# Selected attention on one core: score products between the steps of a weight chunk, a third turning buffer, and one chunk moved forward

## The chip, the cores and the metric

The kernel runs on one core of one Trainium2 chip. The metric is the device time of one launch in microseconds, the median of three runs; lower is better.

## The reference, cut to what matters

Two transformer blocks are computed for 512 tokens of width 1024 in fp32. The part around the change is in the second block: attention over compressed blocks and over selected and windowed keys (with 512 tokens all blocks are selected), eight query heads in two key groups.

```python
q = rmsnorm(q.reshape(b, s, G, R, dh), q_norm_g) * (dh ** -0.5)
s_c = jnp.einsum('bsgrd,bcgd->bgrsc', q, kc).astype(jnp.float32) + bias_c
p_c = masked_softmax(s_c, dist_c >= 0, axis=-1)
o_cmp = jnp.einsum('bgrsc,bcgd->bsgrd', p_c, vc)
```

The selected and the windowed branch do the same with their own keys and values, and a gate sums the three. Beside it, and independent of it, `h @ w_in` is needed for the RWKV projections (14 column tiles) and for two gates (16 column tiles).

## The kernel before, in words

Everything is written by hand, engine by engine; each engine runs its list in order and waits on semaphores.

**Weights come in chunks.** A chunk is 128 output columns of a weight matrix, 128 x 1024 values. SyncE loads it into one of four places of `w_raw` (L332), GpSimd splits it into `w_hi` and `w_lo` (L444, L446), and `chunk` on TensorE (L520 to L536) multiplies it in eight steps of three 512-column matmuls: L531, L532, L533. `chunk` can call a function `also` after each step.

**Fills.** The 30 chunks of the RWKV projections and the gates (f0 to f29) are spread as `fill` calls (L758) over the attention stage and the start of the RWKV stage. ScalarE copies each result out in `fill_out` (L1375, copy L1385) and stores it to DRAM (L1387).

**Units.** The attention has eight units (n, g): query tile n = 0 to 3, key group g = 0, 1. For unit u:

- `nsa_scores` (L837) makes ten products, i = 0 to 9. The first eight (L846) contract 64 rows: a query head (`qn`) against 128(n+1) key columns (`kd`). Heads alternate between partitions 0 to 63 and 64 to 127. Products 8 and 9 (L853) are against the compressed keys, two small matmuls each. The fp32 matmul is issued as two passes, so the trace has two records for each matmul. Four banks take the products in turn; product i waits until VectorE has masked product i - 4 (L843).
- VectorE adds bias and mask in `nsa_mask` (L1962, L1970), ScalarE takes the exponentials (L1441, L1447), and VectorE scales by the weights in `nsa_weights` (L1995, L1998). VectorE's order is weights of u, then mask of u + 1.
- `nsa_weigh` (L861) takes the 2(n+1) + 1 key tiles of the unit one by one: `turn_item` transposes four heads (L879), ScalarE copies the bank to `p2T` (L1462), and `sum_item` multiplies with the values (L893). There are two banks (4 and 5) and two places in `p2T`, and TensorE turns one item ahead.

The order on TensorE is set by this loop:

```python
nsa_scores(*units[0], 0)
fill()
for u, (n, g) in enumerate(units):
    if u + 1 < len(units):
        nsa_scores(*units[u + 1], u + 1)
    fill()
    nsa_weigh(n, g, u)
```

ScalarE follows with the exponentials of u + 1, the copy of the fill, then the copies of u. Before the loop stands one `fill` (f13, L833), behind it `fill(3)`, four `lora` products (L920, L921), `fill(1)`, `head_sums(0)` (L927, L930) and `fill(3)`; then the RWKV scores (L952), which wait for the last fill to be copied (L1058). The last `LATE` = 7 fills go to banks and places of their own (`late_stage`).

Of the kernel before, what the change touches and what calls it, by code (L numbers as in the profile page):

```python
# [78 lines left out]
RW_GROUPS = ((0, 2), (2, 5), (5, 8), (8, 11), (11, 14))  # L79


NFILL, LATE = 14 + 2 * KD, 7
NUNIT = 2 * NT
NORMS = (("ffn1", KD), ("mix", KD), ("pool", 4), ("attn", 4), ("ffn2", KD), ("nsa", KD), ("conv", KD))
RSQRTS = (("ffn1_in", 1), ("ffn1_post", 1), ("mix_in", 1), ("pool_in", 1), ("attn_in", 1), ("wout_post", 1),
# [30 lines left out]
def build(nc, x, positions, params, const, mix_const, w_pool, w_ffn1_gu, w_ffn1_down, w_in, w_out, w_ffn2_gu,  # L116
          w_ffn2_down, w_nsa, nsa_const, rel_bias, distance_code, cmp_pe, cmp_w1, cmp_w2,
          w_rwkv, rwkv_const, rwkv_w2a2, rwkv_g2, w_gates, w_merge, w_out_2, w_conv_up, w_conv_down, out):
    with ExitStack() as ctx:
# [99 lines left out]
        with ExitStack() as scope:  # L219

            with ExitStack() as early:
                def in_e(name, shape, dt=F32):
                    return early.enter_context(nc.sbuf_tensor(name, shape, dt))
                zn = in_e("zn", [P, 11, S])
                pair = in_e("pair", [P, 2, 2, S // 2])
                code = in_e("code", [33, 5 * P])
                rv = in_e("rv", [NH, 5 * P])


            cmp_blocks = [zn[:, a:a + 2, :].rearrange("p a b -> p (a b)")[:, 0:32 * NCMP]  # L230
                          .rearrange("p (j g b) -> p j g b", j=16, g=2) for a in (4, 2)]
            E = in_a("E", [P, 2, 8, S])
            with ExitStack() as early:
                cw1 = early.enter_context(nc.sbuf_tensor("cw1", [P, 16, CMP_H], F32))


            toeplitz = in_a("toeplitz", [P, NH, S])
            qn = in_a("qn", [P, 4, S])
            kd = in_a("kd", [P, 4, S])
            v2_tok = in_a("v2_tok", [P, 2, NT, P])  # L240
            p2T = in_a("p2T", [P, 2, 4, P])
            oA = in_a("oA", [P, 4, S])
            ncs = in_a("ncs", [P, 4 * P])
# [12 lines left out]

            stat = in_a("stat", [P, 2, 3, 12])

        def fill_bank(f):

            return 4 + f % 4 if f < 14 else 7 if f < NFILL - LATE else (0, 1, 2, 4, 5, 3, 0)[f - NFILL + LATE]

        def by_tile(x):
            return x.rearrange("p (n t) -> p n t", n=NT)
# [253 lines left out]
        @block.tensor  # L518
        def _(pe):
            def chunk(c, s, k0, k1, rhs_hi, rhs_lo, dst, start, stop, each=None, w0=None, also=None,  # L520
                      shift=0):


                w0 = k0 if w0 is None else w0
                pe.wait_ge(*nth("w_split", c + 1))
                for k in range(k0, k1):
                    if each:
                        pe.wait_ge(*nth(each, k + 1 + shift))
                    hi = w_hi[:, s, (k - w0) * P:(k - w0 + 1) * P]
                    lo = w_lo[:, s, (k - w0) * P:(k - w0 + 1) * P]  # L530
                    nc.tensor.matmul(dst, hi, rhs_hi[:, k, :], start=start and k == k0, stop=False)  # L531
                    nc.tensor.matmul(dst, hi, rhs_lo[:, k, :], start=False, stop=False)  # L532
                    last = nc.tensor.matmul(dst, lo, rhs_hi[:, k, :], start=False, stop=stop and k == k1 - 1)  # L533
                    if also:
                        also(k)
                return last  # L536
# [218 lines left out]

            filled = [0]

            def fill(n=1):  # L758

                for f in range(filled[0], filled[0] + n):  # L760
                    if f == NFILL - 1:
                        pe.wait_ge(*nth("fill_read", NFILL - LATE + 1))
                    elif 4 <= f <= NFILL - LATE:
                        pe.wait_ge(*nth("fill_read", f - 3 if f < 14 else f))
                    chunk(FIRST["rwkv"] + f, (FIRST["rwkv"] + f) % RING, 0, KD, h_hi, h_lo,
                          bank[fill_bank(f)][:, :], True, True).then_inc(sem("w_used"), 1)
                filled[0] += n

            pe.wait_ge(*nth("zn_read", 11))
# [34 lines left out]
            for v in range(2):  # L804
# [21 lines left out]
                else:  # L826
# [3 lines left out]
                                                    cw2[:, 1, h, 0:HD], start=(h == 0), stop=(h == 1),  # L830
                                                    skip_group_check=True)
                    last.then_inc(sem("nsa_job"), 1)
            fill()  # L833
            pe.wait_ge(*nth("nsa_read", 17))
            pe.wait_ge(*nth("kc_normed", 1))

            def nsa_scores(n, g, unit):  # L837


                for i in range(10):  # L840
# [20 lines left out]
            def nsa_weigh(n, g, unit):  # L861
# [8 lines left out]

                def turn_item(x):
                    v, j = items[x]
                    k = turn[0] + x
                    if k >= 2:
                        pe.wait_ge(*nth("p2T_ready", k - 1))
                    for h in range(4):
                        src = Ec[:, unit % 2, h, 0:8 * n + 7] if v == 2 else E[:, unit % 2, 4 * v + h, j * P:(j + 1) * P]
                        rows = 8 * n + 7 if v == 2 else P
                        last = nc.tensor.transpose(bank[4 + k % 2][0:rows, h * P:(h + 1) * P], src, flip)  # L879
                    last.then_inc(sem("nsa_turned"), 1)  # L880

                def sum_item(x):
# [3 lines left out]
                    for h in range(4):  # L886
                        e, i = h % 2, h // 2
                        if v == 2:
                            lhs, rhs = vct[0:8 * n + 7, g, :], p2T[0:8 * n + 7, k % 2, h, :]
                        else:  # L890
                            lhs, rhs = v2_tok[:, v, j, 64 * g:64 * g + 64], p2T[:, k % 2, h, :]
# [4 lines left out]
                    return last  # L896

                turn_item(0)
                for x in range(len(items)):
                    if x + 1 < len(items):  # L900
                        turn_item(x + 1)
                    last = sum_item(x)
                turn[0] += len(items)

            units = [(n, g) for n in range(NT) for g in range(2)]
            nsa_scores(*units[0], 0)
            fill()
# [295 lines left out]
        def _(act):  # L1203
# [209 lines left out]
            for v in range(2):  # L1413
# [13 lines left out]
                else:  # L1427
# [4 lines left out]
                    fill_out(2)  # L1432

            logs()

# [17 lines left out]
            def nsa_copies(n, g, unit):  # L1453
                items = 2 * (n + 1) + 1
                c0 = 2 * P * (unit % 2)
                for x in range(items):
                    k = turn[0] + x
                    act.wait_ge(*nth("nsa_turned", k + 1))
                    if k >= 2:
                        act.wait_ge(*nth("p2T_used", k - 1))  # L1460
                    rows = 8 * n + 7 if x == items - 1 else P
                    nc.scalar.activation(p2T[0:rows, k % 2, :, :].rearrange("p h t -> p (h t)"),  # L1462
                                         bank[4 + k % 2][0:rows, :], ACT.Copy).then_inc(sem("p2T_ready"), 1)
# [65 lines left out]
            decays(0)  # L1529
            fill_out(1)  # L1530
            key_norm(0)
            fill_out(3)
            key_rates(1)
            flat = lambda x: x.rearrange("p a b -> p (a b)")

# [839 lines left out]
```

## Time and profile before

| | |
|---|---|
| median of three runs | 2064.92 us (2062.79 to 2067.34) |
| the profiled execution | 2061.17 us |
| its span | 2059.4 us |
| TensorE busy | 1906.2 us (93%) |
| VectorE busy | 859.3 us (42%) |
| ScalarE busy | 426.5 us (21%) |
| GpSimd busy | 1278.9 us (62%) |
| chain that ended last | PE 82%, DVE 12%, ACT 3% |

The profile gives the busy time of each engine, the chain of work that ended last, the waits, and each instruction with its start. Times in the rows are from the start of the span. PE is TensorE's matmuls, PEld its weight loads, DVE VectorE, ACT ScalarE, POOL GpSimd. A matmul record's length is longer than the distance to the next, since matmuls are pipelined; costs are read from starts. The attention units lie between 1190 and 1344 us.

### The profile page before, as it was taken

Reading aid. Unit: us, or ns where it says so; the run is one execution under the profiler, and the core shown is the slowest. Engines: PE = TensorE matmul, PEld = TensorE weight load, DVE = VectorE, ACT = ScalarE, POOL = GpSimd, SP = SyncE. Lnnn points to the kernel's source line nnn. Section 1 sums busy time; section 2 is a strip of 40 time slices with the busy share of each in tenths; the row PEclk is TensorE's granted clock in tenths of the full one; section 3 lists DMA queues with packets and bytes.
Section 4 is the critical chain, followed back from the end, with each engine's and each line's share of the span. In section 5 each row is a group of like instructions: output and inputs, shape, how many; then the busy total and the mean of one; then the engine's idle time right before and its main releaser. Section 6 shows DMA issues by size and latency. Waiting matters only on the chain.

```text
span 2059.4 us, 29817 instructions
## 1 busy us (share of the span) xinstructions
PE 1906.2 (93%) x11700; PEld 1482.6 (72%) x11700; DVE 859.3 (42%) x1426; ACT 426.5 (21%) x862; POOL 1278.9 (62%) x619
## 2 busy tenths in 40 slices
PE   7999999888779999999799989997868799999998
PEld 5888888656557888888477866676755678888887
DVE  4333321267664333311404244357756635555301
ACT  3000000123431000000213145534431021111100
POOL 6888877734066888877375442333364667777773
PEclk9999999989989999999899999999968999999999
DMA  4222223311022222233242421140023222223231
GB/s 149 92 92 98 93 86 94 118 35 59 11 82 72 92 92 93 92 96 97 99 160 98 160 100 53 42 149 8 4 109 112 72 82 92 92 92 93 91 95 59
DMA packets 58780, 180.33 MB, mean 88 GB/s; under 512 B 6931, under 2 KB 13843, under 8 KB 58172
## 3 DMA queue, kind: packets, MB, share of 16 engines
q1 hardware_dynamic: 49132, 165.83, 24.0%
q10 hardware_dynamic: 9552, 13.13, 1.8%
q8 instruction: 72, 1.18, 0.2%
q14 instruction: 24, 0.20, 0.0%
HBM read 165.81 MB, written 13.13 MB: 87 GB/s over the span
## 4 chain that ended last, share of the span: by engine, by line
PE 82%; DVE 12%; ACT 3%; issue 2%; DMA 0%; ACTq 0%; POOL 0%; DVEq 0%; SPq 0%; POOLq 0%
PE bank L531 23%; PE bank L533 23%; PE bank L532 23%; PE bank L893 1%; DVE h_lo L1643 1%; PE bank L846 1%; PE bank L581 1%; PE bank L879 1%; DVE xT L1690 1%; DVE tmp L1687 1%; DVE sq L2205 1%; PE bank L810 1%; DVE m_lo L2206 1%; DVE sq L2202 1%; PE bank L1051 1%
## 5 line engine op out<-in xcount | busy, mean ns | idle before, releaser
L444 POOL TENSOR_TENSOR w_hi<-w_raw,one 128x1024 fp32r<-128x1024 f32 (+1 forms) x279 | 527.1, 1889 | 595.1 <-PE bank L533 584.0
L446 POOL TENSOR_TENSOR w_lo<-w_raw,w_hi 128x1024 fp32r<-128x1024 f32 (+1 forms) x279 | 696.4, 2496 | 21.9
L531 PE MATMUL bank<-h_hi,w_hi 128*128 128x512 f32 x1528 | 628.1, 411 | 26.6 <-DVE h_lo L1643 12.5
L532 PE MATMUL bank<-h_lo,w_hi 128*128 128x512 f32 x1528 | 606.8, 397 | 0.0
L533 PE MATMUL bank<-h_hi,w_lo 128*128 128x512 f32 x1528 | 606.5, 397 | 0.0
L531 PEld LDWEIGHTS bank<-h_hi,w_hi 128*128 128x128 f32 x1528 | 288.8, 189 | 119.5 <-issue 27.9
L532 PEld LDWEIGHTS bank<-h_lo,w_hi 128*128 128x128 f32 x1528 | 289.3, 189 | 76.0 <-issue 9.8
L533 PEld LDWEIGHTS bank<-h_hi,w_lo 128*128 128x128 f32 x1528 | 288.8, 189 | 70.5
L531 PE MATMUL bank<-a_hi,w_hi 128*128 128x512 f32 x528 | 208.6, 395 | 0.0
L532 PE MATMUL bank<-a_lo,w_hi 128*128 128x512 f32 x528 | 208.6, 395 | 0.0
L533 PE MATMUL bank<-a_hi,w_lo 128*128 128x512 f32 x528 | 208.6, 395 | 0.0
L1680 DVE TENSOR_TENSOR acc<-acc,sq 128x512 f32<-128x512 f32 x16 | 30.5, 1906 | 214.8 <-ACT sq L1263 214.8
L1254 ACT ACTIVATE tmp<-tmp 128x512 f32<-128x512 f32 x44 | 27.8, 632 | 440.0 <-DVE tmp L1654 440.0
L531 PEld LDWEIGHTS bank<-a_hi,w_hi 128*128 128x128 f32 x528 | 99.1, 188 | 24.2
L533 PEld LDWEIGHTS bank<-a_hi,w_lo 128*128 128x128 f32 x528 | 99.1, 188 | 24.1
L532 PEld LDWEIGHTS bank<-a_lo,w_hi 128*128 128x128 f32 x528 | 99.1, 188 | 24.0
L1654 DVE TENSOR_TENSOR tmp<-bank,rstd 128x512 f32<-128x512 f32 x44 | 30.4, 691 | 139.2 <-PE bank L533 130.6
L1662 DVE TENSOR_TENSOR a_hi<-tmp,bank 128x512 f32 x44 | 30.3, 688 | 139.1 <-PE bank L533 139.1
L492 POOL TENSOR_TENSOR OT<-mats,rcs 128x256 f32<-128x256 f32 x40 | 33.4, 847 | 78.7 <-DVE mats L2112 67.2
L1616 ACT ACTIVATE tmp<-bank,prm 128x512 f32<-128x512 f32 x44 | 34.3, 780 | 154.6 <-DVE bank L2228 154.6
L1657 DVE TENSOR_TENSOR tmp<-tmp,rstd 128x512 f32<-128x512 f32 x44 | 47.3, 1074 | 31.4 <-ACT tmp L1254 31.4
L1263 ACT ACTIVATE sq<-bank 128x512 f32<-128x512 f32 x16 | 9.6, 598 | 237.1 <-PE bank L533 237.1
(342 smaller groups left out, 2116.0 us busy)
## 6 DMA issues: line engine op xcount, KB each, us to landing
w_raw<-w_ffn_gu_dram SPq DMA_DIRECT2D x88, 512.0 KB, 3.4
w_raw<-w_conv_up_dram SPq DMA_DIRECT2D x44, 512.0 KB, 3.5
w_raw<-w_ffn_down_dram SPq DMA_DIRECT2D x32, 448.0 KB, 3.2
w_raw<-w_ffn_down_dram SPq DMA_DIRECT2D x16, 512.0 KB, 3.5
w_raw<-w_out_dram SPq DMA_DIRECT2D x16, 512.0 KB, 3.5
w_raw<-w_gates_dram SPq DMA_DIRECT2D x16, 512.0 KB, 3.5
w_raw<-w_rwkv_dram SPq DMA_DIRECT2D x14, 512.0 KB, 3.4
w_raw<-w_conv_down_dram SPq DMA_DIRECT2D x16, 448.0 KB, 3.3
```

The source lines that it names most:

```text
L444: nc.gpsimd.tensor_tensor(w_hi[:, s, 0:width], raw, one[:, 0:1].to_broadcast([P, width]), ALU.mult).then_inc(sem("w_rounded"), 1)
L446: nc.gpsimd.tensor_tensor(w_lo[:, s, 0:width], raw, w_hi[:, s, 0:width].bitcast(F32), ALU.subtract).then_inc(sem("w_split"), 1)
L492: nc.gpsimd.tensor_tensor(OT[:, k % 2, units_of(half), :] .rearrange("p (n e) t -> p n e t", e=2), mats[:, 2 * half:2 * half + 2, :, 0, :] ...
L531: nc.tensor.matmul(dst, hi, rhs_hi[:, k, :], start=start and k == k0, stop=False)
L532: nc.tensor.matmul(dst, hi, rhs_lo[:, k, :], start=False, stop=False)
L533: last = nc.tensor.matmul(dst, lo, rhs_hi[:, k, :], start=False, stop=stop and k == k1 - 1)
L1254: nc.scalar.activation(tmp[:, u, :], tmp[:, u, :], ACT.Silu).then_inc(sem(tag + "_silu"), 1)
L1616: nc.scalar.activation(tmp[:, v, :], bank[2 * u + v][:, :], ACT.Identity, bias=bias, scale=w)\
L1654: nc.vector.tensor_tensor(tmp[:, u, :], bank[2 * u][:, :], rstd[:, :], ALU.mult)\
L1657: nc.vector.tensor_tensor(tmp[:, u, :], tmp[:, u, :], rstd[:, :], ALU.mult)\
L1662: nc.vector.tensor_tensor(hi, tmp[:, u, :], bank[2 * u + 1][:, :], ALU.mult)\
L1680: nc.vector.tensor_tensor(acc[:, :], acc[:, :], sq[:, m % 2, :], ALU.add).then_inc(sem(tag + "_acc"), 1)
```

## The change

It has three parts.

1. In units 1 to 7, only score products 0 and 1 stand ahead of the fill. Products 2 to 9 are called through `also`, one after each of the eight steps of the chunk. So that the chunk's semaphore still counts the chunk, `chunk` gets an option `count`.
2. The turning of key tiles is three deep: banks 4, 5 and 0, three places in `p2T`, and TensorE turns two items ahead. Since bank 0 also takes scores, the third turn waits until all scores of the next unit are masked.
3. `fill(2)` stands ahead of unit 0 in place of `fill()`, and the last `fill(3)` becomes `fill(2)`; `LATE` is 6. Every chunk in the units has a number one higher. ScalarE's `fill_out` calls move with them.

```diff
-NFILL, LATE = 14 + 2 * KD, 7
+NFILL, LATE = 14 + 2 * KD, 6
...
-            p2T = in_a("p2T", [P, 2, 4, P])
+            p2T = in_a("p2T", [P, 3, 4, P])
...
+                    if count and k == k1 - 1:
+                        last.then_inc(sem("w_used"), 1)
                     if also:
                         also(k)
...
-            fill()
+            fill(2)
             pe.wait_ge(*nth("nsa_read", 17))
             pe.wait_ge(*nth("kc_normed", 1))
...
-                    if k >= 2:
-                        pe.wait_ge(*nth("p2T_ready", k - 1))
+                    if x >= 3:
+                        pe.wait_ge(*nth("p2T_ready", turn[0] + x - 2))
+                    elif x == 2:
+                        pe.wait_ge(*nth("nsa_masked", 10 * min(unit + 2, NUNIT)))
...
                 turn_item(0)
+                turn_item(1)
                 for x in range(len(items)):
-                    if x + 1 < len(items):
-                        turn_item(x + 1)
+                    if x + 2 < len(items):
+                        turn_item(x + 2)
                     last = sum_item(x)
...
-            nsa_scores(*units[0], 0)
+            nsa_scores(*units[0], 0, range(10))
             fill()
             for u, (n, g) in enumerate(units):
                 if u + 1 < len(units):
-                    nsa_scores(*units[u + 1], u + 1)
-                fill()
+                    nsa_scores(*units[u + 1], u + 1, range(2))
+                    fill(also=lambda k: nsa_scores(*units[u + 1], u + 1, range(k + 2, k + 3)))
+                else:
+                    fill()
                 nsa_weigh(n, g, u)
...
             head_sums(0)
-            fill(3)
+            fill(2)
```

TensorE before, at the end of the weighing of unit 1 and through the scores of unit 3 (`kd`, `qn` are keys and queries, `kcn` the compressed keys, `vct` their values):

```order
L893 MATMUL bank<-p2T,vct 64x128 [waits p2T_ready]
L893 MATMUL bank<-p2T,vct 64x128 x3
L846 MATMUL bank<-kd,qn 128x256 [waits masked] x8
L853 MATMUL bank<-kcn,qn 128x15 [waits masked]
L853 MATMUL bank<-kcn,qn 128x15
L853 MATMUL bank<-kcn,qn 128x15 [waits masked]
L853 MATMUL bank<-kcn,qn 128x15
L531 MATMUL bank<-h_hi,w_hi 128x512 [waits w_split,fill_read]
L532 MATMUL bank<-h_lo,w_hi 128x512
```

The same place in the changed kernel, whose lines are numbered a little higher (L848 is the score product, L533 to L535 the chunk's three matmuls, L896 the sum):

```order
L896 MATMUL bank<-p2T,vct 64x128 [waits p2T_ready]
L896 MATMUL bank<-p2T,vct 64x128 x3
L848 MATMUL bank<-kd,qn 128x256 [waits masked] x2
L533 MATMUL bank<-h_hi,w_hi 128x512 [waits w_split,fill_read]
L534 MATMUL bank<-h_lo,w_hi 128x512
L535 MATMUL bank<-h_hi,w_lo 128x512
L848 MATMUL bank<-kd,qn 128x256 [waits masked]
L533 MATMUL bank<-h_hi,w_hi 128x512
```

Six of the eight 64-row products that stood in one run now stand one by one between groups of three 128-row matmuls; the two compressed products follow the last two steps.

TensorE in the changed kernel, from the last step of a chunk into the weighing of a unit with three key tiles:

```order
L535 MATMUL bank<-h_hi,w_lo 128x512
L855 MATMUL bank<-kcn,qn 128x15 [waits masked]
L855 MATMUL bank<-kcn,qn 128x15
L882 MATMUL bank<-ncs,E 128x128 [waits nsa_weighed]
L882 MATMUL bank<-ncs,E 128x128 x7
L882 MATMUL bank<-ncs,Ec 7x128 [waits masked]
L882 MATMUL bank<-ncs,Ec 7x128 x3
L896 MATMUL bank<-p2T,v_tok 64x128 [waits p2T_ready]
```

Three turns now stand ahead of the first sum, where there were two, and the last score product stands directly ahead of them.

## Rows read from the trace of the kernel before

**Rows 1.** The page: TensorE's granted clock in 40 slices, tenths of full speed.
```profile
PEclk9999999989989999999899999999968999999999
```
**Rows 2.** The stretches: us, busy time (x instructions) of each engine, PEclk, DMA share, GB/s.
```profile
1198.50:1213.40 14.90, 10.19 (x50) 8.43 (x49) 10.27 (x46) 4.92 (x25) 4.45 (x2) 0.77 0.16 54
1213.40:1344.10 130.70, 122.39 (x890) 87.91 (x888) 50.02 (x229) 71.73 (x207) 38.97 (x16) 1.00 0.16 51
```
**Rows 3.** What TensorE's L846 waited for: us, times.
```profile
  DVE stat L1962: 18.1, 24
```
**Rows 4.** TensorE, unit 1: start us, length us, instruction [idle before <-releaser].
```profile
1198.54 0.71 PE L846 MATMUL bank<-kd,qn 64*128 64x128 f32 x8
1203.96 1.43 PE L846 MATMUL bank<-kd,qn 64*128 64x128 f32 x8 [4.71 <-DVE stat L1962]
```
**Rows 5.** TensorE, scores of units with n = 1, 2 and 3.
```profile
1231.34 1.13 PE L846 MATMUL bank<-kd,qn 64*128 64x256 f32 x8
...
1234.94 0.51 PE L531 MATMUL bank<-h_hi,w_hi 128*128 128x512 f32 x1
...
1247.35 4.02 PE L846 MATMUL bank<-kd,qn 64*128 64x384 f32 x16
...
1251.97 0.50 PE L531 MATMUL bank<-h_hi,w_hi 128*128 128x512 f32 x1
...
1283.77 4.98 PE L846 MATMUL bank<-kd,qn 64*128 64x512 f32 x16
1288.23 1.24 PE L853 MATMUL bank<-kcn,qn 64*128 64x31 f32 x8
1289.40 0.50 PE L531 MATMUL bank<-h_hi,w_hi 128*128 128x512 f32 x1
```
**Rows 6.** TensorE, from 128-row matmuls to 64-row products.
```profile
1360.73 0.40 PE L533 MATMUL bank<-h_hi,w_lo 128*128 128x512 f32 x1
1361.05 0.69 PE L920 MATMUL bank<-pin,w2a 64*128 64x512 f32 x1
...
1361.59 0.59 PE L920 MATMUL bank<-pin,w2a 64*128 64x512 f32 x1
...
1362.02 0.59 PE L920 MATMUL bank<-pin,w2a 64*128 64x512 f32 x1
```
**Rows 7.** TensorE, from 64-row products (256 columns) back to 128-row matmuls.
```profile
507.80 0.38 PE L608 MATMUL bank<-k_rot,q_rot 64*128 64x256 f32 x2
...
508.45 0.39 PE L532 MATMUL bank<-h_lo,w_hi 128*128 128x512 f32 x1
```
**Rows 8.** TensorE, a 128-row fp32 product (L581) between chunk steps.
```profile
615.77 1.02 PE L581 MATMUL bank<-sq,cst 128*128 128x512 f32 x2
...
617.34 1.02 PE L581 MATMUL bank<-sq,cst 128*128 128x512 f32 x2
```
**Rows 9.** TensorE, weighing of unit 5 (n = 2).
```profile
1294.87 0.39 PE L533 MATMUL bank<-h_hi,w_lo 128*128 128x512 f32 x1
1295.11 1.03 PE L879 MATMUL bank<-ncs,E 128*128 128x128 f32 x8
1297.01 0.66 PE L893 MATMUL bank<-p2T,v_tok 128*64 128x128 f32 x8 [0.87 <-ACT p2T L1462]
1297.60 0.66 PE L879 MATMUL bank<-ncs,E 128*128 128x128 f32 x4
```
**Rows 10.** ScalarE, last exponential, copy of the fill, first copies of unit 5.
```profile
1292.35 0.30 ACT L1447 ACTIVATE Ec<-Ec,stat 128x31 f32<-128x31 f32 x1
...
1295.30 0.60 ACT L1385 ACTIVATE stage<-bank 128x512 f32<-128x512 f32 x1 [2.56 <-PE bank L533]
...
1296.36 1.09 ACT L1462 ACTIVATE p2T<-bank 128x512 f32<-128x512 f32 x2 [0.46 <-PE bank L879]
```
**Rows 11.** VectorE's last step ahead of the RWKV scores, and TensorE's first score.
```profile
1380.86 0.16 DVE L2080 COPY PC<-decay 128x8 f32<-128x8 f32 x1
...
1392.26 0.45 PE L952 MATMUL bank<-AR,KK 64*64 64x128 f32 x8 [0.69 <-ACT late_stage L1385]
```

More of the change, by code:

```diff
@@ L259, in fill_bank @@
         def fill_bank(f):
-            return 4 + f % 4 if f < 14 else 7 if f < NFILL - LATE else (0, 1, 2, 4, 5, 3, 0)[f - NFILL + LATE]
+            return 4 + f % 4 if f < 14 else 7 if f < NFILL - LATE else (0, 1, 2, 4, 5, 3)[f - NFILL + LATE]
+        TURN_BANKS_NSA = (4, 5, 0)
         def by_tile(x):
@@ L520, in chunk @@
             def chunk(c, s, k0, k1, rhs_hi, rhs_lo, dst, start, stop, each=None, w0=None, also=None,
-                      shift=0):
+                      shift=0, count=False):
                 w0 = k0 if w0 is None else w0
@@ L756, in _, with fill @@
             filled = [0]
-            def fill(n=1):
+            def fill(n=1, also=None):
                 for f in range(filled[0], filled[0] + n):
-                    if f == NFILL - 1:
-                        pe.wait_ge(*nth("fill_read", NFILL - LATE + 1))
-                    elif 4 <= f <= NFILL - LATE:
+                    if 4 <= f <= NFILL - LATE:
                         pe.wait_ge(*nth("fill_read", f - 3 if f < 14 else f))
                     chunk(FIRST["rwkv"] + f, (FIRST["rwkv"] + f) % RING, 0, KD, h_hi, h_lo,
-                          bank[fill_bank(f)][:, :], True, True).then_inc(sem("w_used"), 1)
+                          bank[fill_bank(f)][:, :], True, True, also=also, count=True)
                 filled[0] += n
@@ L832, in _, with nsa_scores @@
                     last.then_inc(sem("nsa_job"), 1)
-            fill()
+            fill(2)
             pe.wait_ge(*nth("nsa_read", 17))
             pe.wait_ge(*nth("kc_normed", 1))
-            def nsa_scores(n, g, unit):
-                for i in range(10):
+            def nsa_scores(n, g, unit, some):
+                for i in some:
                     b = bank[i % 4] if unit % 2 == 0 else bank[(i + 2) % 4]
@@ L872, in turn_item @@
                     v, j = items[x]
-                    k = turn[0] + x
-                    if k >= 2:
-                        pe.wait_ge(*nth("p2T_ready", k - 1))
+                    if x >= 3:
+                        pe.wait_ge(*nth("p2T_ready", turn[0] + x - 2))
+                    elif x == 2:
+                        pe.wait_ge(*nth("nsa_masked", 10 * min(unit + 2, NUNIT)))
                     for h in range(4):
@@ L878, in turn_item @@
                         rows = 8 * n + 7 if v == 2 else P
-                        last = nc.tensor.transpose(bank[4 + k % 2][0:rows, h * P:(h + 1) * P], src, flip)
+                        last = nc.tensor.transpose(bank[TURN_BANKS_NSA[x % 3]][0:rows, h * P:(h + 1) * P], src, flip)
                     last.then_inc(sem("nsa_turned"), 1)
@@ L888, in sum_item @@
                         if v == 2:
-                            lhs, rhs = vct[0:8 * n + 7, g, :], p2T[0:8 * n + 7, k % 2, h, :]
+                            lhs, rhs = vct[0:8 * n + 7, g, :], p2T[0:8 * n + 7, x % 3, h, :]
                         else:
-                            lhs, rhs = v2_tok[:, v, j, 64 * g:64 * g + 64], p2T[:, k % 2, h, :]
+                            lhs, rhs = v2_tok[:, v, j, 64 * g:64 * g + 64], p2T[:, x % 3, h, :]
                         last = nc.tensor.matmul(dst[64 * e:64 * e + 64, i * P:(i + 1) * P], lhs, rhs,
@@ L1431, in _ @@
                         .then_inc(sem("toeplitz_in"), 16)
-                    fill_out(2)
+                    fill_out(3)
             logs()
@@ L1458, in nsa_copies @@
                     act.wait_ge(*nth("nsa_turned", k + 1))
-                    if k >= 2:
-                        act.wait_ge(*nth("p2T_used", k - 1))
+                    if x >= 3:
+                        act.wait_ge(*nth("p2T_used", k - 2))
                     rows = 8 * n + 7 if x == items - 1 else P
-                    nc.scalar.activation(p2T[0:rows, k % 2, :, :].rearrange("p h t -> p (h t)"),
-                                         bank[4 + k % 2][0:rows, :], ACT.Copy).then_inc(sem("p2T_ready"), 1)
+                    nc.scalar.activation(p2T[0:rows, x % 3, :, :].rearrange("p h t -> p (h t)"),
+                                         bank[TURN_BANKS_NSA[x % 3]][0:rows, :], ACT.Copy).then_inc(sem("p2T_ready"), 1)
                 turn[0] += items
@@ L1531, in _ @@
             key_norm(0)
-            fill_out(3)
+            fill_out(2)
             key_rates(1)
```

## The prediction

> **What bounds the kernel now.** I read the page first, for where TensorE is idle; then the stretches around the attention units, its waits, and its instructions one by one. TensorE is busy for 93% of the span and the chain is 82% its own, so a change in this stage is worth what TensorE's list gets shorter or longer. Through units 1 to 7 its clock is at the full level of 2.4 GHz (1.00) from 1213.40 on, and it is busy 122.39 of 130.70 us; ahead of that stands a stretch of 14.90 us with 10.19 busy and a clock of 0.77 [rows 1, 2]. Its L846 waits for masks, 18.1 us in 24 waits [rows 3], counted from its weight loads. One wait of 4.71 us makes a quarter of that: in unit 1, mask 0 stands on VectorE behind the weights of unit 0 [rows 4]. The other 23 share 13.4 us, and they lie inside runs of products that go on in pairs. The reader is to see that removing such a wait gains only what the product then costs less than before.
>
> **What a run of products costs now.** From the first product to the chunk's first matmul it is 3.60 us for n = 1, 4.62 for n = 2 and 5.63 for n = 3 [rows 5]. Each stands twice, so 27.7 us for units 2 to 7, waits included.
>
> **What a product costs between two steps.** Three things.
>
> - Its passes. A pass of 512 columns over 64 rows takes 0.43 us (1361.59 to 1362.02), and in that row two passes of the two halves start together, 64 rows each [rows 6]. A product alone has no partner, so it pays both its passes: 0.43, 0.64 and 0.86 us for n = 1, 2, 3, and 0.21 for n = 0.
> - Going from 128 rows to 64. L533 starts at 1360.73, the second pass of L920 at 1361.59; less 0.23 for L533 and 0.43 for the first pass, 0.20 us are left [rows 6].
> - Going back. The last 256-column pass starts at 507.80, L532 at 508.45; less 0.21 for the pass and 0.23 for L531, 0.21 us are left [rows 7].
>
> A product over all 128 rows does not pay this: with L581 behind each step the period is 1.56 us, three matmuls of 0.23 and two passes of 0.43, and nothing over [rows 8]. So it is the change of rows that costs, and I bound it by these rows: from 0 (as L581) to 0.41 us. I take 0.40, since the changed list has exactly the two passages of rows 6 and 7. A product alone is then 0.83, 1.04 and 1.26 us for n = 1, 2, 3, and 0.61 for n = 0. The two compressed products take 1.17 us together with one passage back [rows 5], 0.58 each; with both passages of its own I take 0.75.
>
> The Trainium skill ("TensorE: Matmul & The Clock Gate", section "Part 3: Packing small matmuls", "The mechanism") says that a weight load is pulled ahead of running matmuls when it goes to another row group or to the background weight buffer. By the second half a passage would cost nothing, and the sum would come out as in the first rival below. The rows contradict it for the change of rows: 0.20 us each way [rows 6, 7].
>
> **Scores, units 2 to 7.** The first two products stay together: 0.63, 0.84 and 1.06 us to the chunk (a pass pair of 0.21, 0.32 or 0.43 us twice, and 0.2). Then six alone and two compressed:
>
> - n = 1: 0.63 + 6 x 0.83 + 1.5 = 7.1 against 3.60
> - n = 2: 0.84 + 6 x 1.04 + 1.5 = 8.6 against 4.62
> - n = 3: 1.06 + 6 x 1.26 + 1.5 = 10.1 against 5.63
>
> Twice each: 51.6 against 27.7, **+23.9 us**. No mask wait is left: a step and a product take 1.5 us or more, and even with their waits the eight products of n = 3 took 4.46 us, 0.56 each [rows 5], so the masks keep a pace far below that.
>
> **Unit 1.** From its first product to the first turn 14.90 us passed [rows 2]. Now: pair 0.42, chunk 5.6 (24 x 0.233), six products 3.7, two compressed 1.5, sum 11.2. Product 4 must wait for mask 0, which still stands behind unit 0's weights: its start is 5.42 us after the first product [rows 4], and TensorE gets there after 0.42 + 3 x 0.70 + 2 x 0.61 = 3.7. So 1.7 us of the wait stay: 12.9, **-2.0 us**. The clock of 0.77 there should go back to 1.00, since the gap gets a third as long; with the drop it would be 14.
>
> **Turning.** Now the first sum starts 2.14 us behind the chunk's last matmul (1294.87 to 1297.01), with two turns ahead of it: the fill's copy, its store and the first copy to `p2T` stand in a row on ScalarE, and TensorE waits 0.87 us [rows 9, 10]. In the change the exponentials of the last product come ahead of that copy, where they were 2.2 us early before [rows 10]. Behind the chunk's last matmul: 0.9 until product 9 is out, 0.5 for its masks, 0.7 for two exponentials, then 0.6 + 0.46 + 0.65 to the first copy's end: 3.8 us. Of that, 0.75 is counted as the product, and 0.58 is the third turn that is made in it. 3.8 - 2.14 - 0.75 - 0.58 = 0.35, over seven units **+2.4**. Unit 7 has no product in its chunk: 2.14 is almost filled by three turns of 0.58, **-0.7**. At each unit's end 0.15 us for the last copy go, **-1.2**. In between nothing is to be gained: a turn and a sum take 1.17 us, a copy 0.6 [rows 9, 10]. The third turn's wait for masks is over by then (1.4 us behind the chunk, against 2.1).
>
> **The moved chunk.** Behind f13 stands f14, which waits for f13's copy. A copy starts 0.43 us behind the last matmul and lasts 0.60 [rows 9, 10]; the next matmul would come at 1.1 instead of 0.23: **+0.9**. The chunk itself is 5.6 us earlier here and 5.6 less ahead of the RWKV scores. It comes back there: VectorE is ready at 1381.02, TensorE's fills end at 1392 [rows 11], so even 5.6 us earlier TensorE is last by 5. ScalarE's copy and store move with it, beside TensorE. SyncE's loads and GpSimd's splits keep their order, and are a chunk further ahead. If that cover were gone, up to 5.6 us would be lost.
>
> **Sum.** 23.9 - 2.0 + 2.4 - 0.7 - 1.2 + 0.9 = +23.3 us. The profiled execution of before took 2061.17, 3.75 under the median of the runs; against itself the sum gives 2084.5, against the median **2088**.
>
> **Rivals.**
>
> 1. *The passages cost nothing*, as with L581 [rows 8]. The six products then cost their passes and the compressed ones 0.45: 4.1, 5.6 and 7.1 us, twice each 33.6 against 27.7, +5.9. In unit 1 it is 0.42 + 5.6 + 1.3 + 0.9 + 2.5 of wait = 10.7, -4.2. With +1.4 for the rest: +3, 2068, no change that can be told. Against it: rows 6 and 7. Chance 0.07.
> 2. *The products are cheaper than in the runs*, the way of the change that ends faster. It decides at the price of 27.7 / 60 = 0.46 us a product: if one between steps costs less than that beside its chunk, the removed waits count. At half the passes, as in a pair, and no passage: 2.3, 3.2 and 4.1 us, twice each 19.2 against 27.7, -8.5; unit 1 9.9 against 14.9, -5.0; rest +1.4: -12, 2053. It would need a 64-row pass to run beside the chunk's 128-row matmuls. For it: halves run side by side [rows 6]. Against it: a chunk's matmul takes both halves. Chance 0.05.
> 3. *The clock falls*. If TensorE's wait of about 1.1 us ahead of each first sum, up from 0.87, took it to 1.2 GHz, seven falls like the one behind the 4.71 us wait, at 2 to 3 us each, would add 14 to 21: 2102 to 2109. Against it: the waits of 0.87 [rows 9] left the clock at 1.00 [rows 2]. Chance 0.05.
> 4. *The moved chunk does not come back*, since something else releases the RWKV scores: +5.6, 2094. Against it: rows 11. Chance 0.05.
>
> **How the numbers follow.** The forecast, 2088, has 0.78. About 0.2% (4 us) is what a measurement of this kernel can tell from no change. Faster by more: rival 2 and half of what I can't name, 0.06. Within: rival 1, 0.07. Slower: the rest, 0.87. The range: a passage price halved takes 56 x 0.2 = 11 us off, 2077; allowing for some of the rival with free passages, 2068. Above, rival 4 gives 2094, and some further wait on ScalarE of 0.5 to 1 us a unit 2100. Rival 2 and most of rival 3 stay outside.
>
> **What would show it.** L846's waits for masks fall from 18.1 to about 2 us, and yet units 2 to 7 get longer: from first product to first turn 12.7, 14.2 and 15.7 us for n = 1, 2, 3, where it was 9.3, 10.3 and 11.3. L532 follows 0.34, not 0.23, behind each L531 that has a product ahead of it. First sum 3.8 us behind the chunk's last matmul. Stretch from the last sum to the RWKV scores 5.6 shorter. Wrong would be: a period of step and product of 1.56 us or less at n = 3 (rival 1), or a clock under 1.00 between units 2 and 7.

## The result, and the profile after

The changed kernel takes 2084.95 us, the median of four runs (2081.95 to 2085.5), against 2064.91 before: 20.0 us more, a ratio of 1.0094 with the interval 1.0076 to 1.0111. The forecast was 2088 us, slower, with 2068 to 2100 as its range. The profiled execution has a span of 2083.7 us.

The page after: busy times, and the granted clock in 40 slices.

```profile
PE 1929.2 (93%) x11700; PEld 1478.0 (71%) x11700; DVE 872.1 (42%) x1426; ACT 429.9 (21%) x862; POOL 1274.5 (61%) x619
...
PEclk9999999999989999999999999999978899999999
```

TensorE has the same 11,700 matmuls and is busy 23 us longer. The clock is not the cause: the units' slices show nines, as in [rows 1], and unit 1, at 0.77 before [rows 2], is now at 1.00, as the rows below show. The stretches of unit 1, of the weighing of unit 0 up to that of unit 7, and from there to the RWKV scores (us, busy time (x instructions) of PE, PEld, DVE, ACT, POOL, then PEclk, DMA share, GB/s):

```profile
1205.99:1218.67 12.68, 11.32 (x50) 6.99 (x49) 7.43 (x27) 4.80 (x21) 4.87 (x3) 1.00 0.19 62
1218.67:1370.70 152.03, 143.65 (x890) 86.11 (x889) 69.83 (x248) 75.70 (x211) 33.61 (x16) 1.00 0.12 41
1370.70:1413.30 42.60, 40.01 (x170) 28.96 (x168) 26.16 (x36) 16.49 (x25) 10.99 (x5) 1.00 0.46 173
```

The middle stretch is the 130.7 us of [rows 2]: 21.3 us longer, with the same number of matmuls. The first was 14.9 us, the last 48.2. So the loss lies between units 2 and 7, and there TensorE is busy with it. The timeline of TensorE in unit 6 (n = 3) shows what with, against [rows 5]:

```profile
1302.88 1.13 PE L848 MATMUL bank<-kd,qn 64*128 64x512 f32 x4
1303.93 0.50 PE L533 MATMUL bank<-h_hi,w_hi 128*128 128x512 f32 x1
1304.27 0.40 PE L534 MATMUL bank<-h_lo,w_hi 128*128 128x512 f32 x1
1304.51 0.39 PE L535 MATMUL bank<-h_hi,w_lo 128*128 128x512 f32 x1
1304.83 1.12 PE L848 MATMUL bank<-kd,qn 64*128 64x512 f32 x2
1305.88 0.50 PE L533 MATMUL bank<-h_hi,w_hi 128*128 128x512 f32 x1
1306.22 0.39 PE L534 MATMUL bank<-h_lo,w_hi 128*128 128x512 f32 x1
```

From one lone product to the next (1304.83 to 1306.77) a step takes 1.95 us. Three matmuls of 0.233 are 0.70 of it and two passes 0.86; the other 0.39 are the two passages. They show in three places: 0.09 ahead of the product (L535 to L848 takes 0.32 where L534 to L535 takes 0.23), 0.19 in the product and behind it (1304.83 to L533 at 1305.88 is 1.05, with two passes of 0.43 in it), and 0.11 behind the first matmul (L533 to L534 takes 0.34). The periods for n = 1 and 2 are 1.52 and 1.73 us.

The weight loads of the same stretch show what a passage is:

```profile
1304.04 0.19 PEld L534 LDWEIGHTS bank<-h_lo,w_hi 128*128 128x128 f32 x1
1304.27 0.19 PEld L535 LDWEIGHTS bank<-h_hi,w_lo 128*128 128x128 f32 x1
1304.83 0.29 PEld L848 LDWEIGHTS bank<-kd,qn 64*128 64x128 f32 x2 [0.36 <-issue]
1305.88 0.19 PEld L533 LDWEIGHTS bank<-h_hi,w_hi 128*128 128x128 f32 x1 [0.76 <-issue]
```

The loads of L534 and L535 begin 0.23 us ahead of their own matmuls (1304.27 and 1304.51), while the matmul ahead runs. The loads of the lone product and of the L533 behind it begin together with their matmuls, so nothing hides them.

The stage adds up, before to after, by the starts in the two timelines:

| | before | after | difference | forecast |
|---|---|---|---|---|
| last compressed-value product to scores of unit 0 | 6.36 | 12.91 | +6.55 | +6.5 |
| unit 1, first product to first turn | 14.86 | 12.68 | -2.2 | -2.0 |
| units 2 to 7, the same, sum | 61.9 | 84.8 | +22.9 | +23.9 |
| weighings, sum of eight | 63.03 | 61.47 | -1.6 | +0.5 |
| last sums to the RWKV scores | 48.78 | 43.19 | -5.6 | -5.6 |
| | | | +20.1 | +23.3 |

The forecasts of the first and last rows are the moved chunk's 5.6 us and its 0.9 of waiting. The two single spans differ by 24.3 us, 4.2 more than this: 0.9 arises before the stage and 3.3 behind the start of the RWKV scores. From there to the end it is 667.1 us before and 670.4 after, and in the ten traces below it is 668.4 to 672.2, with or without the moved chunk. The medians differ by 20.0, so I read those 4.2 as the spread between executions.

### The profile page after: what moved, and what is told of

It is laid out like the page before. It is cut to its first block, busy times and chain, and to the rows that moved or that the text cites. A ratio compares the mean times of both kernels' runs of the same rounds, so it can differ in the third digit from the quotient of the medians.

```text
span 2083.7 us, 29794 instructions
## 1 busy us (share of the span) xinstructions
PE 1929.2 (93%) x11700; PEld 1478.0 (71%) x11700; DVE 872.1 (42%) x1426; ACT 429.9 (21%) x862; POOL 1274.5 (61%) x619
## 4 chain that ended last, share of the span: by engine, by line
PE 82%; DVE 13%; ACT 3%; issue 2%; POOL 0%; DMA 0%; ACTq 0%; DVEq 0%; SPq 0%; POOLq 0%
PE bank L533 24%; PE bank L535 23%; PE bank L534 23%; PE bank L848 2%; PE bank L896 1%; PE bank L585 1%; DVE h_lo L1650 1%; DVE sq L2212 1%; DVE m_lo L2213 1%; PE bank L812 1%; PE bank L882 1%; DVE xT L1697 1%; DVE tmp L1694 1%; PE bank L1058 1%; DVE sq L2209 1%
## 5 line engine op out<-in xcount | busy, mean ns | idle before, releaser
L533 PE MATMUL bank<-h_hi,w_hi 128*128 128x512 f32 x1528 | 632.1, 414 | 28.5 <-DVE h_lo L1650 12.9
L534 PE MATMUL bank<-h_lo,w_hi 128*128 128x512 f32 x1528 | 605.7, 396 | 0.0
L535 PE MATMUL bank<-h_hi,w_lo 128*128 128x512 f32 x1528 | 605.3, 396 | 0.0
L533 PEld LDWEIGHTS bank<-h_hi,w_hi 128*128 128x128 f32 x1528 | 288.0, 189 | 144.8 <-issue 51.4
L534 PEld LDWEIGHTS bank<-h_lo,w_hi 128*128 128x128 f32 x1528 | 288.4, 189 | 74.1 <-issue 10.0
L535 PEld LDWEIGHTS bank<-h_hi,w_lo 128*128 128x128 f32 x1528 | 288.2, 189 | 70.8
L535 PE MATMUL bank<-a_hi,w_lo 128*128 128x512 f32 x528 | 208.3, 395 | 0.0
L533 PE MATMUL bank<-a_hi,w_hi 128*128 128x512 f32 x528 | 208.3, 394 | 0.0
L534 PE MATMUL bank<-a_lo,w_hi 128*128 128x512 f32 x528 | 208.3, 394 | 0.0
L533 PEld LDWEIGHTS bank<-a_hi,w_hi 128*128 128x128 f32 x528 | 98.9, 187 | 24.5
L534 PEld LDWEIGHTS bank<-a_lo,w_hi 128*128 128x128 f32 x528 | 98.9, 187 | 24.2
L535 PEld LDWEIGHTS bank<-a_hi,w_lo 128*128 128x128 f32 x528 | 98.9, 187 | 24.2
```

## The experiments

Two theories stood against each other at first: that a lone product pays passages and a partner that it no longer has, and that a third buffer, a moved chunk or the interrupted chunk carries the loss. Intervals are of the ratio to the kernel before.

**Scores back in one run.**

```diff
-                    nsa_scores(*units[u + 1], u + 1, range(2))
-                    fill(also=lambda k: nsa_scores(*units[u + 1], u + 1, range(k + 2, k + 3)))
-                else:
-                    fill()
+                    nsa_scores(*units[u + 1], u + 1, range(10))
+                fill()
```

> The change with its first part undone: all ten score products stand ahead of the chunk again; three-deep turning and the moved chunk stay. Theory (passages between 128 and 64 rows, and lone products): units 2 to 7 fall back to 9.3, 10.3 and 11.3 us from first product to first turn (n = 1, 2, 3), unit 1 to 14.9. The third turn now fills TensorE's wait ahead of the first sum, so each weighing is 0.5 to 0.65 us shorter than in the kernel before, 4 to 5 us in all, less 0.95 for the moved chunk: 2061 us, 4 under before. Rival (the three-deep turning or the moved chunk carries the loss): 2080 or more.

Measured: 2058.87 us, 0.9967 (0.9953 to 0.998). First product to first turn is 9.30, 10.33 and 11.33 us again, and 15.35 in unit 1. TensorE's timeline at the first sum of unit 5 (n = 2; the bracket is the wait and what ended it):

```profile
1299.10 1.47 PE L882 MATMUL bank<-ncs,E 128*128 128x128 f32 x12
1300.95 0.66 PE L896 MATMUL bank<-p2T,v_tok 128*64 128x128 f32 x8 [0.37 <-ACT p2T L1466]
```

Three turns are made in the time in which TensorE made two and waited 0.87 us [rows 9]; 0.37 is left. Each weighing is 0.8 to 0.95 us shorter, more than the 0.65 expected. So the first part of the change costs 26 us on top of the other two, and these two together gain 6.

**Interleaving alone.** The first part of the change applied to the kernel before; two-deep turning, no chunk moved.

```diff
-                    nsa_scores(*units[u + 1], u + 1)
-                fill()
+                    nsa_scores(*units[u + 1], u + 1, range(2))
+                    fill(also=lambda k: nsa_scores(*units[u + 1], u + 1, range(k + 2, k + 3)))
+                else:
+                    fill()
```

> The kernel before with the first part of the change alone: products 2 to 9 between the steps of the chunk, two-deep turning, no chunk moved. Theory: +22.9 us in units 2 to 7 and -2.2 in unit 1, as in the changed kernel; the first sum comes 3.55 us behind the chunk's last matmul with only two turns ahead of it, +0.86 us in each of seven units, +6: 2091 to 2092 us, slower than the change itself. Rival (the three parts share the loss): at or under the change's 2085.

Measured: 2090.78, 2098.67, 2120.16 and 2121.89 us, 1.0217 (1.0139 to 1.0294). The theory's 2091 is the fastest of them, and the spread was not expected. The two slow ones have a mean granted clock of 0.946 and 0.948 over the whole run, the other two 0.967 and 0.964. The profiled run (2098.67) shows where it comes from, here unit 4's chunk and the weighing behind it, then the next pair, by stretches:

```profile
1254.60:1271.50 16.90, 15.31 (x60) 7.84 (x56) 6.48 (x27) 8.42 (x28) 3.01 (x2) 1.00 0.01 5
1271.50:1277.80 6.30, 6.16 (x52) 4.17 (x52) 4.32 (x12) 2.28 (x4) 1.24 (x1) 0.73 0.31 113
1277.80:1294.60 16.80, 15.25 (x58) 7.84 (x56) 6.44 (x27) 8.38 (x28) 2.96 (x2) 1.00 0.07 21
1294.60:1303.30 8.70, 8.52 (x76) 5.94 (x76) 4.36 (x12) 3.51 (x7) 1.28 (x1) 0.80 0.28 84
```

and TensorE's timeline at the start of the second stretch:

```profile
1271.55 0.69 PE L895 MATMUL bank<-p2T,v_tok 128*64 128x128 f32 x8 [1.65 <-ACT p2T L1467]
1272.17 1.12 PE L881 MATMUL bank<-ncs,E 128*128 128x128 f32 x4
```

TensorE waits 1.65 us ahead of the first sum, and right behind it the same four transposes take 1.05 us to the next row instead of 0.59: the clock is at half. Behind the waits of 1.64 to 1.69 us in the weighings of units 3 to 6 it fell four times, and each of these weighings is about 1.5 us longer for it than it would be at 1.00; behind 1.61 in units 1 and 2 it did not fall. That is the third rival of the prediction. At 0.87 before and 1.1 to 1.2 in the changed kernel the clock stayed at 1.00. The third turning buffer takes 0.49 off this wait where it is tried alone (0.87 to 0.38, below), which is the distance between the changed kernel and this one. That the runs of 2120 us are more of such falls is likely from their clock, but no trace shows one.

**Products in pairs.** An even and an odd head together behind each second step.

```diff
-                    fill(also=lambda k: nsa_scores(*units[u + 1], u + 1, range(k + 2, k + 3)))
+                    fill(also=lambda k: nsa_scores(*units[u + 1], u + 1, range(k + 1, k + 3) if k % 2 else ()))
```

> The change with its products between the steps in pairs, one even and one odd head together: two after each second step, in place of one after each. Theory: half the passages, and the two passes of a pair run side by side, so three pairs cost what three lone products did: from first product to first turn 9.7, 10.5 and 11.4 us for n = 1, 2, 3 (12.6, 14.1 and 15.6 in the change), unit 1 10.4 in place of 12.7. Total 2061 us. Rival 1 (each step that is interrupted costs by its wait on a mask, pairs or not; the pair does not run side by side): 2073 or more. Rival 2 (a product costs its columns alone): no change from 2085.

Measured: 2066.55 us, 1.0001 (0.999 to 1.0011). First product to first turn: 9.45, 10.3 and 11.17 us where the clock was whole, and 10.24 in unit 1, each a little under the theory. The pairs of unit 6 follow each other like this:

```profile
1291.80 1.13 PE L848 MATMUL bank<-kd,qn 64*128 64x512 f32 x4
...
1294.45 1.13 PE L848 MATMUL bank<-kd,qn 64*128 64x512 f32 x4
...
1297.11 1.13 PE L848 MATMUL bank<-kd,qn 64*128 64x512 f32 x4
```

2.65 us from pair to pair, less 1.40 for two steps, is 1.25 us for two products; a lone one cost 1.25 (1.95 less 0.70). Beside its partner the second product of a pair is free. The total missed by 5.5 us for another reason: both compressed products now come behind the last step, and their masks and four exponentials with them, so the wait ahead of the first sum grew to 1.63 to 1.8 us (12.4 in all, against 8.4), and the clock fell behind two of them (0.84 in unit 2's chunk, 0.85 in the weighing of unit 5) and not behind the five others.

**All products over 128 rows.** In this kernel each score product sums two heads, so the attention is another one; columns, order and waits are the same.

```diff
-                                                qn[64 * e:64 * e + 64, 2 * g + h // 2, n * P:(n + 1) * P],
-                                                kd[64 * e:64 * e + 64, 2 * (i // 4) + g, 0:(n + 1) * P],
+                                                qn[:, 2 * g + h // 2, n * P:(n + 1) * P],
+                                                kd[:, 2 * (i // 4) + g, 0:(n + 1) * P],
```

> The change with every score product over all 128 rows in place of 64, so each sums two heads and the attention's values are others; columns, waits and order are the same. Theory (the change of rows costs 0.4 us a product): lone products cost their passes alone, 0.43, 0.64 and 0.86 us for n = 1, 2, 3, compressed ones 0.45; first product to first turn 9.9, 11.6 and 13.3 us (the first two products no longer run side by side), unit 1 10.7. Total 2068 us, with the period of step and product 1.13, 1.34 and 1.56 us. Rival (the passage cost belongs to the wait or to the kind of matmul, fp32 between rounded ones, not to the rows): period stays 1.52, 1.73 and 1.95 us, total 2087.

Measured: 2069.84 us, 1.0018 (1.0009 to 1.0028). The lone products of unit 6:

```profile
1292.05 1.02 PE L848 MATMUL bank<-kd,qn 128*128 128x512 f32 x2
...
1293.61 1.02 PE L848 MATMUL bank<-kd,qn 128*128 128x512 f32 x2
...
1295.17 1.02 PE L848 MATMUL bank<-kd,qn 128*128 128x512 f32 x2
```

The period is 1.56 us, that of [rows 8], against 1.95 with 64 rows. Twice the rows, and 0.39 us less a product: the passage belongs to the change of rows, not to the wait on a mask nor to fp32 between rounded matmuls. First product to first turn is 9.95, 11.66 and 13.37 us, as the theory has it. Fifteen of the 20 us of loss go with it, although the first two products lose their side-by-side run.

**Three-deep turning alone.** The kernel before with the second part of the change (its three buffers of `p2T` and its waits, as in the diff ahead of the prediction), and no more:

```diff
                 turn_item(0)
+                turn_item(1)
                 for x in range(len(items)):
-                    if x + 1 < len(items):
-                        turn_item(x + 1)
+                    if x + 2 < len(items):
+                        turn_item(x + 2)
                     last = sum_item(x)
```

> The kernel before with the three-deep turning alone: scores in one run, no chunk moved. Theory: the third turn fills 0.5 us of TensorE's 0.87 us wait ahead of each first sum and the wait for the last copy goes, as in the run with the scores in one run (2058.9 us), and the 0.95 us that the second chunk waits for its copy is not paid: 2058 us. Rival (the gain came from the moved chunk): 2064 or more.

Measured: 2056.14 us, 0.996 (0.9946 to 0.9974). The moved chunk gains nothing: with it the time was 2058.87 (0.9967). The table above has it at +0.95, and the two intervals overlap, so its price is read from the traces and not from these times.

**Copies first.** ScalarE copies the fill out behind its first three copies to `p2T`, in the changed kernel and in the one with interleaving alone.

```diff
-                fill_out()
                 nsa_copies(n, g, u)
...
+                    if x == 2:
+                        fill_out()
```

> The change with ScalarE's copy of the fill moved behind its first three copies to p2T. Theory: ahead of the first sum ScalarE's chain is 1.06 us shorter (0.60 copy, 0.46 store), so TensorE's wait of 1.1 to 1.2 us there nearly goes in seven units, 0.4 in the eighth: -7.5 to -8, 2077 us. Rival (the exponentials alone hold the first copy back): within 2 us of 2085.

Measured: 2077.35 us, 1.0062 (1.0045 to 1.0079), as expected. The row being moved, ScalarE between the chunk with unit 6's scores and unit 5's first sum in the changed kernel, and TensorE's side of it:

```profile
1319.31 0.30 ACT L1454 ACTIVATE Ec<-Ec,stat 128x31 f32<-128x31 f32 x1
...
1319.62 0.57 ACT L1392 ACTIVATE stage<-bank 128x512 f32<-128x512 f32 x1
...
1320.59 1.58 ACT L1469 ACTIVATE p2T<-bank 128x512 f32<-128x512 f32 x3 [0.40 <-ACT stage L1392]
```

```profile
1317.64 0.39 PE L535 MATMUL bank<-h_hi,w_lo 128*128 128x512 f32 x1
1317.96 0.63 PE L855 MATMUL bank<-kcn,qn 64*128 64x31 f32 x4
1318.52 1.53 PE L882 MATMUL bank<-ncs,E 128*128 128x128 f32 x12
1321.24 0.55 PE L896 MATMUL bank<-p2T,v_tok 128*64 128x128 f32 x6 [1.19 <-ACT p2T L1469]
```

From 1319.62 to 1320.59 ScalarE works for a chunk that nobody waits for, while TensorE waits 1.19 us for the copy behind it. Without it the waits ahead of the first sums fall from 8.4 to 0.7 us.

> The interleaving alone (two-deep turning), which took 2091 to 2122 us and showed the clock at half behind waits of 1.65 us, with ScalarE's copy of the fill moved behind its first three copies. Theory (the spread comes from the clock, and the clock falls for the waits of 1.65 us): the waits shrink to 0.6 us, the clock stays at its full level from unit 2 to unit 7, and all runs lie at 2081 to 2086 us. Rival (the spread has another cause): runs above 2095 remain.

Measured: 2080.05, 2082.78, 2088.15 and 2090.14 us. The waits fell from 12.3 to 3.8 us, none over 0.64, and from unit 2 on the clock stayed whole in the profiled run; runs of 2120 are gone. That half of the theory stands. But the runs do not keep to 2081 to 2086, and two lie above it: the profiled one, 2090.14, has the clock down in unit 1:

```profile
1207.00:1224.00 17.00, 17.00 (x71) 10.99 (x71) 7.03 (x37) 7.47 (x29) 4.24 (x2) 0.60 0.17 54
1224.00:1370.00 146.00, 141.71 (x843) 82.67 (x840) 64.81 (x230) 72.40 (x203) 29.77 (x14) 1.00 0.14 43
```

In that stretch TensorE is busy without a gap at 0.60. Ahead of it lie a wait of 0.27 us for a copy and the mask wait of 1.10 us in unit 1. The changed kernel has the same two waits at the same places and did not fall in its profiled run. Why it falls here is open.

**Four products ahead, six inside.** Three-deep turning, no chunk moved.

```diff
+                    nsa_scores(*units[u + 1], u + 1, range(4))
+                    at = 5 if u == 0 else 3
+                    fill(also=lambda k: nsa_scores(*units[u + 1], u + 1, range(4, 10) if k == at else ()))
```

> Three-deep turning, no chunk moved, and the ten products in two runs: four ahead of the chunk, which find their banks free, and six after the chunk's step 3 (step 5 in unit 1), when their masks are done. Theory: one more change of rows each way (0.4 us) for a unit, but the waits on masks go and the products stay side by side: from first product to first turn 8.3, 9.2 and 10.1 us for n = 1, 2, 3 (9.3, 10.3, 11.3 before), unit 1 8.3 in place of 14.9: 2045 to 2048 us. Rival (interrupting a chunk costs as such, whatever the products' order): 2064 or more.

Measured: 2048.97 us, 0.9924 (0.9908 to 0.9941). Unit 1 in its timeline, to be read against [rows 4]:

```profile
1200.08 0.71 PE L850 MATMUL bank<-kd,qn 64*128 64x128 f32 x8
...
1205.54 1.12 PE L850 MATMUL bank<-kd,qn 64*128 64x128 f32 x8 [0.24 <-DVE stat L1971]
1206.42 0.82 PE L857 MATMUL bank<-kcn,qn 64*128 64x7 f32 x8
```

The first four products find their banks free, TensorE does six steps while the first mask still stands behind unit 0's weights, and of 4.71 us of wait 0.24 is left; unit 1 takes 8.6 us in place of 14.9. In the other units the gain is small, 0.2 to 0.45 us each where 1.0 was expected: 9.08, 9.99 and 10.9 us. The second run has two compressed products of 1.17 us at its end, and I had priced these at 0.5.

**The split in unit 1 only.** Three-deep turning, every other unit's products in one run.

```diff
+                if u == 0:
+                    nsa_scores(*units[1], 1, range(4))
+                    fill(also=lambda k: nsa_scores(*units[1], 1, range(4, 10) if k == 5 else ()))
+                else:
+                    if u + 1 < len(units):
+                        nsa_scores(*units[u + 1], u + 1, range(10))
+                    fill()
```

> Three-deep turning, no chunk moved, and only unit 1's products in two runs (four ahead of the chunk, six after its step 5); units 2 to 7 keep one run. Theory: the run with all units split took 2049.0 us against 2056.1 without; its trace gives 6.2 us of that to unit 1 (8.7 in place of 14.9 us from first product to first turn), less 0.8 for a longer wait ahead of its first sum, and 1.9 to the six other units: 2050.7 us. Rival (the split pays in every unit alike): 2054 or more.

Measured: 2053.79 us (2051.4 to 2058.09), 3 over the theory and as good as at the rival's 2054; the trace has to decide. Units 3 to 7 are as in three-deep turning alone (9.30, 10.32 and 11.33 us), and unit 1 takes 8.6, so the gain of unit 1 is there. It is lost again in unit 2: TensorE gets there 5.4 us earlier than in three-deep turning alone, but VectorE begins unit 1's weights no earlier (18.2 us behind the first score product, against 18.1). With unit 2's products in one run TensorE then waits for the first mask, and the clock falls to 0.75 in the stretch behind:

```profile
1213.85 1.73 PE L850 MATMUL bank<-kd,qn 64*128 64x256 f32 x8 [1.70 <-DVE stat L1972]
```

```profile
1211.00:1224.90 13.90, 12.20 (x51) 9.71 (x49) 8.78 (x51) 5.59 (x25) 0.21 (x1) 0.75 0.12 38
```

13.9 us where 9.3 is the rule. VectorE is late because one of its steps in the weights of unit 1, 0.23 us long in the kernel before, takes 2.39 here. It ends when an instruction of GpSimd ends that splits the next chunk's weights:

```profile
1208.84 2.39 DVE L2002 TENSOR_SCALAR stat<-stat,prm 128x4 f32<-128x4 f32 x1
1208.86 2.35 POOL L448 TENSOR_TENSOR w_lo<-w_raw,w_hi 128x1024 fp32r<-128x1024 f32 x1
```

The kernel with all units split has the same long step, and no wait in unit 2: its split gives VectorE the time. So the split of the following unit is worth more than its own 0.2 us.

**Split and copies first.** The kernel with all units split, and the copies first as above:

```diff
                     nc.scalar.activation(p2T[0:rows, x % 3, :, :].rearrange("p h t -> p (h t)"),
                                          bank[TURN_BANKS_NSA[x % 3]][0:rows, :], ACT.Copy).then_inc(sem("p2T_ready"), 1)
+                    if x == 2:
+                        fill_out()
```

> All units split (four products ahead, six inside the chunk), three-deep turning, and ScalarE's copy of the fill moved behind its first three copies to p2T. Theory: the eight waits ahead of the first sums, 3.9 us in all, go, and nothing else changes: 2045 us. Rival (they are hidden elsewhere, or the later copy of the fill holds a chunk back): 2049.

Measured: 2047.48 us (2046.86 to 2048.29), 0.9913 (0.9897 to 0.993). The eight waits ahead of the first sums went from 3.9 to 0.2 us, the time from 2048.97 by 1.5, which is too little for two medians to tell apart (the ratios are 0.9913 and 0.9924, their intervals overlap). The traces say more: from unit 0's first product to the RWKV scores it is 187.34 us without and 183.60 with the copies first, 3.7 less, so the waits were not hidden elsewhere, although a mask wait of 0.36 us came up in unit 3. It is the fastest version here, 17.4 us under before by the medians shown and 37.5 under the change.

## Why the prediction was right

**The direction and the place.** Right: TensorE's own list got longer. The lone products were forecast at 0.83, 1.04 and 1.26 us, measured 0.82, 1.03 and 1.25 (periods of 1.52, 1.73 and 1.95 less 0.70). Both parts of the price are shown, the passages by the kernel over 128 rows, the missing partner by the pairs. The phases came out at 12.6, 14.1 and 15.6 against 12.7, 14.2 and 15.7. That is 1.0 us less than forecast for the six units, most of it from the last compressed product, put at 0.75 and measured 0.65 (L535 at 1317.64 to the first turn at 1318.52, less 0.23).

**Unit 1.** Right: 12.68 against 12.9, with 1.10 us of wait seen ahead of L848 where 1.7 was forecast, 0.27 of wait for the fill's copy that was not in the sum, and the clock whole. What the prediction did not ask is why mask 0 is so late. The eight scalings that stand ahead of it on VectorE take 5.53 us in unit 0 of the kernel before, the same eight 1.65 in unit 1, and in the long case GpSimd's two splitting instructions lie within them:

```profile
1198.16 5.53 DVE L1998 TENSOR_SCALAR E<-E,stat 128x128 f32<-128x128 f32 x8
1209.57 1.65 DVE L1998 TENSOR_SCALAR E<-E,stat 128x128 f32<-128x128 f32 x8
```

```profile
1198.69 1.98 POOL L444 TENSOR_TENSOR w_hi<-w_raw,one 128x1024 fp32r<-128x1024 f32 x1 [4.04 <-PE bank L533]
1200.75 2.47 POOL L446 TENSOR_TENSOR w_lo<-w_raw,w_hi 128x1024 fp32r<-128x1024 f32 x1
```

So 3.9 of the 4.71 us of wait go with this meeting of the two engines. The changed kernel has it too (5.57). No run moves GpSimd's splits, so that this would take the wait away is not shown.

**The moved chunk.** Right: +6.55 in front, -5.6 behind. VectorE was ready at 1407.1 and the RWKV scores began at 1413.28, 6 us later, so TensorE was last as before [rows 11].

**Turning.** Here the sum was off, by 2.1 of its 3.2 us. The chain behind the chunk's last matmul was put at 3.8 us, measured 3.5 to 3.6 (1317.64 to 1321.24 in unit 5), so the step ahead of the first sum is +0.24 in unit 5 where +0.35 was forecast. The rest lies at the units' ends, put at -0.15 and measured -0.31: with three turns in hand the last sums also stand without a turn between them, and that run of sums is shorter (in unit 5 the two sums ahead of the last one take 1.02 us, 1325.90 to 1326.92, where a sum between turns takes 0.59). Unit 7 was put at -0.85 with its end and gave -0.95.

**The reading of the waits.** One expectation was wrong: that L846's mask waits would fall from 18.1 to about 2 us in the view that gave [rows 3]. The same view of the changed kernel gives

```profile
  DVE stat L1969: 15.1, 36
```

though TensorE's matmuls waited for masks only twice, 1.4 us in all (before four times, 5.4):

```profile
PE bank L896 <- ACT p2T L1469: 8.4, 8, 1.2
PE bank L848 <- DVE stat L1969: 1.4, 2, 1.1
PE bank L533 <- ACT stage L1392: 1.0, 2, 0.7
```

The 18.1 us counted the weight loads' idle time, and a load ahead of a lone product stands idle while the matmul over 128 rows runs (0.36 us at 1304.83 in the rows of the loads above; the same 0.36 ahead of the next product, at 1306.77, is put down to L1969). By the matmuls, the kernel before had only 0.7 us of mask waits beside the 4.71, not the 13.4 that the prediction shares among the other 23. The prediction noted that the number came from weight loads and priced nothing by it; it should not have made it a test.

**The rivals.** Free passages: refuted, the period at n = 3 is 1.95 us. Products cheaper than in the runs: refuted by the same. The fallen clock: not in the changed kernel, but shown at waits of 1.64 to 1.69 us with two-deep turning, at 1.5 us a fall where the rival had 2 to 3. It was half a microsecond of wait away, so a chance of 0.05 was on the low side. The moved chunk that does not come back: refuted.

The weight load rule of the Trainium skill ("TensorE: Matmul & The Clock Gate", "Part 3: Packing small matmuls", "The mechanism") holds here in its first half, since products of the two halves run side by side. In its second half, that a load can also go ahead into the background buffer, it does not cover a change from 128 rows to 64 or back: 0.39 us a product were paid for the two passages. Between loads of all 128 rows it does hold: L534's load begins 0.23 us ahead of its matmul, and the period with 128-row products is 1.56 us.

## What to carry to other kernels

Filling a wait with work pays what the work costs in its new place: a matmul over half the rows is cheap only beside its partner in the other half and among its like, so move such products in pairs or in runs, and few times. Count a wait by the matmuls' idle time, not by the weight loads'. When a step is put late on a second engine (here the last exponentials), look what stands behind it on that engine and let the copy that is waited for go first. And when one engine gains time on another, look at the next place where they meet: the split of unit 1 alone moved part of its wait into unit 2.

## What the runs showed of the hardware

- Going from 128-row matmuls to 64-row ones and back costs about 0.39 us the two ways; with 128 rows in both places nothing (periods 1.95 and 1.56 us).
- Two 64-row products on different halves take 1.25 us together, as long as one alone, passages included (512 columns, between 128-row matmuls).
- A weight load over 128 rows began 0.23 us ahead of its matmul when the matmul ahead also had 128 rows, and together with it when that one had 64; a 64-row load behind a 128-row matmul began together with its own matmul too.
- The clock dropped to its half level (1.2 GHz) behind single waits of 1.63 to 1.8 us between long busy stretches, in some units and not in others. With waits of at most 1.3 us it did not fall in any trace from unit 2 on, and a wait of 1.89 us for a mask in unit 1, in the run over 128 rows, left it whole. Interleaving alone spread its runs by 31 us. A fall in unit 1 behind a wait of 1.1 us, in one kernel only, stays unexplained.
- VectorE's scalings within GpSimd's splitting instructions took 5.53 us in place of 1.65, and a single one of four columns 2.39 in place of 0.23, ending with GpSimd's.
